# The second layer's input norm in two halves of three token tiles, with a new order of transposes and weight remainders

## The reference

```python
def rms_norm(x, g):
    xf = x.astype(jnp.float32)
    y = xf * lax.rsqrt(jnp.mean(xf * xf, axis=-1, keepdims=True) + EPS)
    return (y * g.astype(jnp.float32)).astype(x.dtype)

def pre_mod(x, g, shift, scale):
    return rms_norm(x, g) * (1 + scale) + shift

def post_add(x, y, g, gate):
    return x + gate * rms_norm(y, g)

# layer 0, last line of conv_ffn, for x and for the context xc
f = (jax.nn.gelu(a) * b) @ w_down          # 2688 -> 1024
x = post_add(x, f, ffn_post_g[0], g2)
# layer 1
h, hc = pre_mod(x, mix_pre_g[1], sh1, sc1), pre_mod(xc, mix_pre_g[1], csh1, csc1)
q, k, v = split_c(h @ w_qkv, q_g, k_g)     # 1024 -> 16 heads of q, 4 of k, 4 of v, each 64 wide
q, k = apply_rope(q, cos, sin), apply_rope(k, cos, sin)
y = global_latent_attention(q, k_all, v_all) @ w_out
```

## Time and profile before

| what | value |
|---|---|
| time, median of 3 runs | 1525.89 us (1524.79 to 1525.99) |
| the profiled execution's own time | 1522.63 us |
| its span | 1520.9 us |
| mean granted TensorE clock | 0.984 |
| busy: PE, DVE, ACT, POOL | 1439.7, 1034.6, 717.4, 568.1 us |

### The profile page before, as it was taken

The page is one execution under the profiler, slowest core; times in us unless marked ns, Lnnn a source line. Parts: engine busy times, 40 slices in busy tenths (PEclk is TensorE's granted clock), DMA queues, the critical chain, the costliest instruction groups (busy, mean ns, idle before and its releaser), DMA issues.

```text
span 1520.9 us, 21702 instructions
## 1 busy us (share of the span) xinstructions
PE 1439.7 (95%) x7514; PEld 1176.4 (77%) x7514; DVE 1034.6 (68%) x1645; ACT 717.4 (47%) x1245; POOL 568.1 (37%) x509
## 2 busy tenths in 40 slices
PE   4989899999999999999999799899999999999998
PEld 1877567778888888887787578677778888888886
DVE  2368777567688667758889778788876444445445
ACT  3333666444332333224555645688875544443222
POOL 2331545343232222321135323465543444444443
PEclk8999999999999999999999899899999999999999
DMA  8230840222465346334897222010002233333321
GB/s 353 63 98 1 294 178 29 84 98 85 133 184 153 97 138 193 110 111 127 250 249 171 80 70 70 30 41 1 1 23 76 86 107 96 97 96 112 98 96 71
DMA packets 138257, 169.16 MB, mean 111 GB/s; under 512 B 8308, under 2 KB 96632, under 8 KB 137152
## 3 DMA queue, kind: packets, MB, share of 16 engines
q1 hardware_dynamic: 132928, 159.44, 33.0%
q0 software_dynamic: 4608, 8.39, 3.3%
q10 hardware_dynamic: 640, 0.26, 0.1%
HBM read 165.94 MB, written 2.14 MB: 111 GB/s over the span
## 4 chain that ended last, share of the span: by engine, by line
PE 82%; DVE 6%; ACT 4%; DMA 4%; issue 2%; POOL 1%; SPq 0%; POOLq 0%; DVEq 0%; ACTq 0%
PE ps L560 22%; PE ps L561 22%; PE ps L562 22%; PE ps L1567 4%; PE ps L1553 4%; PE ps L1578 2%; PE ps L1580 2%; DMA start_w<-in_ada_w_dram 2%; PE ps L1461 1%; DMA fast_more<-in_ffn_w_down_dram 1%; PE ps L1053 1%; ACT prob L1609 1%; PE ps L923 1%; DMA ada_w<-in_ada_w_dram 1%; POOL prob L1740 0%
## 5 line engine op out<-in xcount | busy, mean ns | idle before, releaser
L552 POOL TENSOR_TENSOR w_lo<-raw,w_hi 128x1024 fp32r<-128x1024 f32 (+1 forms) x116 | 276.1, 2382 | 472.4 <-ACT w_hi L546 472.4
L560 PE MATMUL ps<-hT_hi,w_hi 128*128 128x512 f32 (+1 forms) x1096 | 387.4, 353 | 4.4 <-DVE hT_lo L2018 3.7
L561 PE MATMUL ps<-hT_lo,w_hi 128*128 128x512 f32 (+1 forms) x1096 | 385.0, 351 | 0.0
L562 PE MATMUL ps<-hT_hi,w_lo 128*128 128x512 f32 (+1 forms) x1096 | 382.7, 349 | 0.0
L560 PEld LDWEIGHTS ps<-hT_hi,w_hi 128*128 128x128 f32 x1096 | 207.3, 189 | 41.4 <-DVE hT_lo L2018 5.6
L562 PEld LDWEIGHTS ps<-hT_hi,w_lo 128*128 128x128 f32 x1096 | 206.5, 188 | 28.9
L561 PEld LDWEIGHTS ps<-hT_lo,w_hi 128*128 128x128 f32 x1096 | 207.1, 189 | 26.9
L546 ACT ACTIVATE w_hi<-raw 128x1024 fp32r<-128x1024 f32 (+1 forms) x137 | 142.3, 1041 | 97.4 <-PE ps L562 78.0
L1740 POOL TENSOR_SCALAR prob<-prob,small 128x768 f32<-128x768 f32 (+3 forms) x112 | 90.0, 804 | 122.1 <-DVE small L1658 122.1
L560 PE MATMUL ps<-w_hi,hT_hi 128*128 128x512 f32 (+1 forms) x288 | 110.8, 385 | 6.6 <-DVE hT_lo L895 2.9
L2321 DVE SCALAR_TENSOR_TENSOR conv_b<-ps,convw,conv_b 128x511 f32<-128x511 f32 (+1 forms) x63 | 39.7, 658 | 113.5 <-ACT conv_b L2264 113.5
(11 more groups left out here) (296 smaller groups left out, 2837.0 us busy)
## 6 DMA issues: line engine op xcount, KB each, us to landing
raw<-in_ffn_w_up_dram SPq DMA_DIRECT2D x84, 512.0 KB, 3.9
ada_w_up<-in_ada_w_dram SPq DMA_DIRECT2D x48, 512.0 KB, 4.1
ada_w<-in_ada_w_dram SPq DMA_DIRECT2D x32, 512.0 KB, 4.8
raw<-in_ffn_w_down_dram SPq DMA_DIRECT2D x56, 256.0 KB, 4.3
raw<-in_ffn_w_down_dram SPq DMA_DIRECT2D x21, 512.0 KB, 3.5
fast_more<-in_ffn_w_down_dram SPq DMA_DIRECT2D x38, 256.0 KB, 3.8
start_w<-in_ada_w_dram SPq DMA_DIRECT2D x8, 1024.0 KB, 8.4
raw<-in_ffn_w_down_dram POOLq DMA_DIRECT2D x24, 256.0 KB, 5.7
```

The source lines that it names most:

```text
L552: by.tensor_tensor(split_to(w_lo, phase, m, width), split_from(phase, m, width), split_to(w_hi, phase, m, width).bitcast(F32), ALU.subtrac ...
L560: nc.tensor.matmul(outp, s_hi, m_hi, start=first, stop=False, skip_group_check=True)
L561: nc.tensor.matmul(outp, s_hi, m_lo, start=False, stop=False, skip_group_check=True)
L562: return nc.tensor.matmul(outp, s_lo, m_hi, start=False, stop=last, skip_group_check=True)
```

## The change

- `FAST_TAIL` is 3. In ScalarE's loop `x_scaled` makes xn of tiles 0, 1 and 2 at units 69, 70 and 71. The last two units' weight blocks go to the two `fast_sub` buffers, so that SP can load weight units 0 to 2 of the projection earlier.
- The norm of layer 1 is 16 half-steps (`half_turn`, `half_scalar`, `half_vector`, `half_fill`): 8 chunks for tiles 0 to 2, then 8 for tiles 3 to 5, through two banks. ScalarE writes the high part straight from PSUM and then the scaled value in place; VectorE makes only the remainder. After each half-step PE does the matmuls of three key and value tiles. Half-steps 0 and 1 are transposed ahead of the last product's third tile.
- The first half's parts lie in `first_hi` and `first_lo` (the place of `act_g`), since `hT_hi` and `hT_lo` still hold the product's data. SP moves them into place (two moves of 1.57 MB inside SBUF) ahead of the load of unit 7; the query tiles wait for that.
- Behind the product, ScalarE, VectorE and POOL have new orders: half-steps and weight splits between the steps of the sum back into x (below). Weight remainder 0 is VectorE's, 1 to 3 stay POOL's.
- In the projection the half-steps 8 to 15 stand between the first three key tiles' work; weight remainders 4 to 7 are POOL's, each behind the power of tiles 0 to 3; 8 to 11 are VectorE's as before.
- The transposes get a table in the place of the rule, and the phase waits between norm and projection are gone.

```diff
-FAST_TAIL = 6
+FAST_TAIL = 3
+        def half_turn(pe, step):
+            half, k = divmod(step, KC)
+            if step == 0:
+                pe.wait_ge(s("norm_xn_scalar"), HALF_T)
+                pe.wait_ge(s("fast_out"), OUT_C21 + HALF_T)
+            if step == KC:
+                pe.wait_ge(s("norm_xn_scalar"), HALF_T + 1)
+                pe.wait_ge(s("norm_xn"), norm_base("mix1", "xn") + VECTOR_XN)
+            if step >= 2:
+                pe.wait_ge(s("norm_split"), norm_base("mix1", "split") + 2 * (step - 1))
+            for i in range(HALF_T):
+                mm = nc.tensor.transpose(half_bank(step)[:, i * P:(i + 1) * P],
+                                         xn[:, HALF_T * half + i, k * P:(k + 1) * P], ident[:, :])
+        def half_fill(pe, step):
+            pe.wait_ge(s("norm_split"), norm_base("mix1", "split") + 2 * (step + 1))
...
+            for i in range(HALF_T):
+                mm = mm3(acc_at(1, HALF_T * half + i, width), hi[:, tt], lo[:, tt], ...)
+        def half_scalar(act, step):
+            pieces = ((0, P, 0), (P, HTOK, 1)) if half else ((0, HTOK, 0),)
+            for dst in (half_out(step)[0], half_bank(step)):
+                for c0, c1, v in pieces:
+                    op = nc.scalar.activation(dst[:, c0:c1], half_bank(step)[:, c0:c1], ACT.Identity, ...)
+        def half_vector(dve, step):
+            nc.vector.tensor_tensor(lo, half_bank(step), hi.bitcast(F32), ALU.subtract).then_inc(s("norm_split"), 2)
 proj_sync
+                    if l and m == 7:
+                        sp.wait_ge(s("norm_split"), norm_base("mix1", "split") + 2 * KC)
+                        for whole, first in ((hT_hi, first_hi), (hT_lo, first_lo)):
+                            sp.dma_start(whole[:, :, 0:HTOK].bitcast(F32), first[:, :, :].bitcast(F32))
-        ACC_BANKS = ((0, 1), (6, 7, 4, 5, 0, 1))
-        TURN_LAG = (2, 3)
+        ACC_BANKS = ((0, 1), (6, 5, 4, 7, 0, 1))
+        TURNED_BEHIND1 = {3: (0, 1), 6: (2,), 7: (3,), 8: (4, 5), 9: (6,), 10: (7,), 11: (8, 9), 12: (10,), 13: (11,)}
 proj_tensor, layer 1
+            for step in range(HALF_STEPS if l else 0):
+                half_fill(pe, step)
+                if step + 2 < HALF_STEPS:
+                    half_turn(pe, step + 2)
+                else:
+                    turn(step + 2 - HALF_STEPS)
 proj_scalar, layer 1
+            for step in range(KC, HALF_STEPS if l else 0):
+                half_scalar(act, step)
+                if step in SUMS_AFTER:
+                    read_sums(SUMS_AFTER.index(step))
+                if step in QUERY_HI_AFTER:
+                    split_hi(act, phase, 4 + QUERY_HI_AFTER.index(step), ...)
+        SUMS_AFTER = (KC + 1, KC + 3, KC + 5)
+        QUERY_HI_AFTER = (KC + 4, KC + 6, KC + 7)
+        QUERY_LO_AFTER = {0: (4,), 1: (5,), 2: (6,), 3: (7,),}
+        QUERY_LO_VECTOR = {7: (8, 9, 10), 8: (11,)}
 proj_pool, behind the power of tile n
+                        for m in QUERY_LO_AFTER.get(n, ()):
+                            split_lo(pool, phase, m, unit_width(l, m))
 proj_vector, layer 1 (rope_first: sums, tables, halves; rope_second: factor, QUERY_LO_VECTOR, copy, remainder)
+                half_vector(dve, KC)
+                rope_gains()
+                half_vector(dve, KC + 1)
+                for n in range(HALF_T):
+                    at = rope_first(n)
+                    half_vector(dve, KC + 2 + 2 * n)
+                    if n == HALF_T - 1:
+                        half_vector(dve, KC + 3 + 2 * n)
+                    rope_second(n, at)
+                    if n < HALF_T - 1:
+                        half_vector(dve, KC + 3 + 2 * n)
 fast_tensor, behind the units before the tail
             for i in range(HALF_T):
+                if i == HALF_T - 1:
+                    half_turn(pe, 0)
+                    half_turn(pe, 1)
 fast_scalar, behind the loop
+            close(act, "act")
+            a, b, c = range(HALF_T, ALL_T)
+            whole = len(FAST) - FAST_TAIL + HALF_T
+            weights(0, 2)
+            weights(1, len(FAST) - 4)
+            half_scalar(act, 0)
+            half_scalar(act, 1)
+            second_square(a)
+            second_square(b)
+            x_square(act, "mix1", "ffnpost0", ALL_T, a)
+            second_square(c)
+            weights(2, whole)
+            half_scalar(act, 2)
+            x_square(act, "mix1", "ffnpost0", ALL_T, b)
+            x_scaled(act, "mix1", a)
+            half_scalar(act, 3)
+            x_square(act, "mix1", "ffnpost0", ALL_T, c)
+            weights(3, whole)
+            for step in range(4, KC):
+                half_scalar(act, step)
 fast_vector, behind the loop
+            split_lo(dve, "proj1", 0, unit_width(1, 0), by=nc.vector)
             for t in range(HALF_T):
                 fast_gate_early(dve, HALF_T + t)
-            x_normed(dve, "mix1", 0)
-            x_normed(dve, "mix1", 2)
+            half_vector(dve, 0)
+            half_vector(dve, 1)
             for t in range(HALF_T, ALL_T):
...
                 nc.vector.tensor_tensor(z, fast_second(t), gate[:, v, BANK:D], ALU.mult)
+                if t == ALL_T - 1:
+                    half_vector(dve, 2)
                 added(t)
...
+            half_vector(dve, 3)
+            x_normed(dve, "mix1", ALL_T - 2)
+            half_vector(dve, 4)
             x_normed(dve, "mix1", ALL_T - 1)
+            for step in range(5, KC):
+                half_vector(dve, step)
```

More of the change, by code:

```diff
@@ L434, in norm_base @@
                 return each[what] * ALL_T * len(before)
-            steps = {"mix0": KC, "ffn0": len(norm_steps(0)), "mix1": KC}
+            steps = {"mix0": KC, "ffn0": len(norm_steps(0)), "mix1": HALF_STEPS}
             each = {"turned": 1, "split": 2, "h32": 1}[what]
-            return sum(each * steps[t] * (2 if what == "h32" and t[:3] == "mix" else 1) for t in before)
-        VECTOR_XN = ALL_T - 2
+            return sum(each * steps[t] * (2 if what == "h32" and t == "mix0" else 1) for t in before)
+        VECTOR_XN = ALL_T - 4
+        HALF_STEPS = 2 * KC
         def norm_steps(l):
@@ L937, in norm_tensor, with half_bank, half_out @@
             fill(KC - 1)
+        def half_bank(step):
+            return bank(2 + step % 2, HTOK)
+        def half_out(step):
+            half, k = divmod(step, KC)
+            if half == 0:
+                return first_hi[:, k, :], first_lo[:, k, :]
+            return hT_hi[:, k, HTOK:TOK], hT_lo[:, k, HTOK:TOK]
+        def half_turn(pe, step):
+            half, k = divmod(step, KC)
+            if step == 0:
[9 more added lines that the diff above has]
+                                         xn[:, HALF_T * half + i, k * P:(k + 1) * P], ident[:, :])
+            mm.then_inc(s("norm_turned"), 1)
@@ L1084, in proj_tensor @@
                                 pe.wait_ge(s(f"qk_steps{l}"), free)
-                        for k in range(KC) if gi or batch[0] >= KV_FIRST else ():
+                        if l and gi == 1 and batch[0] == 0:
+                            pe.wait_ge(s("first_moved"), 2 * 16)
+                        for k in range(KC) if gi or l == 0 else ():
                             if batch[0] == 0 and k % 2 == 0:
@@ L2398, in fast_landed @@
                 return
-            name, before = FAST_LANDED[slot]
-            eng.wait_ge(s(name), before + 16 * (u // FAST_RAW + 1))
+            name, before = FAST_LANDED[fast_slot(u)]
+            turns = u // FAST_RAW
+            if u >= FAST_LAST:
+                turns = len(range(u - FAST_LAST, sum(FAST_SUBS), FAST_SUB))
+            eng.wait_ge(s(name), before + 16 * (turns + 1))
         def fast_source(at):
```

258 lines of the change are left out of this document (145 added, 113 removed).

## The result

| | before | after |
|---|---|---|
| time, median, four runs each | 1525.34 us (1522.86 to 1525.99) | 1536.78 us (1535.17 to 1540.09) |
| ratio, 95% interval | | 1.0081 (1.006 to 1.0101) |
| profiled execution, its span | 1522.63, 1520.9 us | 1535.17, 1533.2 us |
| mean granted TensorE clock | 0.984 | 0.983 |

The changed kernel is 11.4 us slower; 1536.5 was forecast, within 1527 to 1541. The page gives the same picture as before: 7514 matmuls, 2.7 us more busy time, 12.3 us more span.

What follows compares the result with a forecast made beforehand. TensorE, busy 95% of the span, was taken as the bound, so only its idle or half-clock stretches matter. Stage costs 2.0 - 0.2 + 8.8 = 10.6 us, added to 1525.9, gave 1536.5 us; range 1527 to 1541.

Steps and rivals of the forecast that it cites:

- The product: End of the last Strassen product: three waits, 2.1 us together against 2.9 before; TensorE through at 855.3, against 856.25.
- First half: Norm half-steps 0 to 7: TensorE idles 7.6 us before half-step 2, then loses 1.6 us at the lower clock.
- Half-step 7: Last half-step of the norm's first half: ends at 883.7, TensorE being the late engine at 2.42 us a step.
- Half-step 13: Norm's second half: tile 1's power waits behind weight remainder 4 on GpSimd; 3.5 us idle, 1.8 at lower clock.
- Up to the batch: Keys' end to the end of query tiles 7 to 9: 24.75 us, against 24.95 before.
- The order of turns: New transpose order behind the query tiles holds VectorE at tile 6; tile 13's sum of squares 8.8 us later.
- The sum: Start of tile 13's last chain: 2.0 - 0.2 + 8.8 = 10.6 us later; time 1536.5.
- Rival 1: GpSimd's remainders 3 and 5 lock out VectorE, adding 0.8 and 0.7 us on TensorE's path; 1538.0; chance 0.1.
- Rival 2: GpSimd doesn't bind half-step 13, so 3.5 and 1.8 us go; +5.3, 1531.2; chance 0.13.
- rival 4: The order of turns costs nothing, VectorE not being held at tile 6; 1528.5; chance 0.12.
- Rival 3: TensorE runs through both norm halves; keys end 13.5 us earlier, 8.6 lost in the queries; 1521.0; chance 0.06.
- What was put at nothing: Costed at nothing: two moves of first_hi and first_lo, 3.1 MB, with 28 us of cover, and removed phase waits.

Runs made afterwards that it cites:

- e2_power: Changed kernel with GpSimd's weight remainder 4 behind the power of tile 1, 5 and 6 behind that of tile 2; 1532.07 us, ratio 1.0051.
- e3_chain: Changed kernel with another order on VectorE and ScalarE behind the last product, the tile chains starting earlier; 1533.31 us, ratio 1.0055.
- e6_chain2: Changed kernel with the order of e3_chain, some half-steps moved further, and weight remainders 1 and 2 by VectorE; 1530.95 us, ratio 1.0045.
- e1_turns: Changed kernel with the old order of turns (transposes behind the query tiles); 1529.11 us, ratio 1.0033.
- e4_before_turns: Kernel before with only the new order of turns behind the query tiles; 1534.54 us, ratio 1.0067.
- v1_all: Changed kernel with e6_chain2's changes, remainders 4 to 7 by VectorE, old turns and a separate table for ScalarE's key readings; 1516.62 us, ratio 0.9951.
- e5_vec_lo: Changed kernel with weight remainders 4 to 7 by VectorE instead of GpSimd; 1532.17 us, ratio 1.0047.

## Why the prediction was right

**The product.** Through at 855.3 forecast, 855.2 measured (855.59 less its wait). The three waits are 1.79 us (0.37, 0.89, 0.53), forecast 2.1. That the instants agree so closely is in part luck: the waiting matmul that A begins with comes at 847.2 to 851.3 in the runs with this same code ahead of it. What was forecast well are the lengths between them.

**First half.** Half-step 2 forecast for 867.75, measured 867.57; chains from 855.84 (856.0), 3.77 apart (3.78). Idle 6.89 where 7.6 stood, as half-steps 0 and 1 ended 0.6 later. The clock was the lower one until 870.6, for the first 6 of the 9 matmuls where 8 were taken; in e2_power, behind the same wait, until 875.4, so this term has 1.5 us of chance in it. The reason behind it, the length of the path over VectorE, ScalarE and GpSimd, was tested by e3_chain and e6_chain2: shortened, it brings half-step 2 from 20.21 to 16.99 and 14.03 us behind the reference matmul.

**Half-step 7** ended at 883.5 (883.7). ScalarE's four activations were taken at 1.7, they take 1.60.

**Half-step 13.** Power of tile 1 done at 898.20 (898.3), matmul at 899.97 (900.1), idle 3.19 (3.5). The lower clock was put at 1.8 us; 0.71 for 3.0 us and 0.87 for 6.5 are 1.7. It fell only 1.3 us after TensorE was back at work; in e1_turns it did not fall at all behind the same wait, so that this term came true is partly luck. The queue as cause is shown by e2_power. Keys end at 908.65 (909.1), so the stage costs 1.5 us, not 2.0. The queue inversion was the right reading of an order of instructions that no row of before shows: only the durations came from rows, the order from the code.

**Up to the batch.** The wait for unit 7 is 1.14 (1.35). The batch ends at 933.97 (934.23 less 0.26), 25.3 after the keys, forecast 24.75; so this stage costs 0.4 where -0.2 stood.

**The order of turns.** Forecast +8.8 for the batch's end to tile 13's sum of squares, 36.9 us; measured 37.7, which is +9.6. Tile 10 starts about 9.1 after the batch (8.65): the mechanism is as said, with the copy of tile 6 held 7.54 us. One term was wrong in kind: the wait of 2.2 us for weight remainder 11 is 0.17. Remainder 11 was there at 948.74, within 0.3 us of the forecast (batch's end + 15.0); it was TensorE that came 1.8 us later than forecast, at 948.47, slowed by the clock. The waits of 4.66 and 1.25 brought the lower clock, 0.50 in 940 to 943 and 0.81 in 943 to 950, the last alone 0.19 x 7 = 1.3 us; with half of the 1.75 us of work in the first it is 2.2. The prediction had counted no clock loss there although it counted one behind the other two stalls. Two errors of nearly one size so cancelled. The last turns ahead of attention (976.39) took 1.97 instead of 1.09 us at the lower clock, 0.9 more that was not forecast.

**The sum.** +10.6 forecast (2.0, -0.2, 8.8); +11.45 measured at tile 13's sum of squares (1.5, 0.4, 9.6, from unrounded instants), +12.3 in span, +11.4 in the medians.

**Rival 1, VectorE locked out,** was given 0.1 and is half true. The mechanism is there. The three gate products ahead of the chains, beside remainder 1, took 4.09 us (850.90) where 1.9 would do; ScalarE had half-step 1 only at 855.19, so the chains began some 0.2 us later for it. At the rival's own places it did not lengthen the path: xn of tile 5 took 2.00 us and one operation of the halves of tile 2 took 1.15 instead of 0.29 (900.94), but TensorE was the late engine there and waited for neither. Its price shows once the larger waits are gone: 0.98 us in e2_power, 1.7 us in the first chain of e3_chain. By the Trainium skill, page "SBUF — State Buffer", section "Who interferes with whom", a VectorE instruction with two SBUF inputs and a GpSimd instruction that reads SBUF hold each other off for a whole instruction. The trace agrees, now with VectorE as the loser (0.42 to 2.37 and 2.50, 0.69 to 2.38), where the earlier trace rows had only GpSimd.

**Rival 2** (GpSimd doesn't bind half-step 13) and **rival 4** (the turns cost nothing) are excluded by e2_power and by e1_turns and e4_before_turns. **Rival 3** (TensorE runs through both halves) was given 1521.0, with the turns' loss in it. In the changed kernel the two stalls exclude it. v1_all, with the turns mended, goes a good half of its way: from the product's end to the end of the keys the rival counted 38.3 us, v1_all takes 43.6, before took 50.9. It needed, as the rival said, other chains than the earlier trace rows, not a faster engine. What was put at nothing (the moves of `first_hi` and `first_lo`, the removed phase waits) is named by no wait in the trace; no run took it out by itself.

## What to carry to other kernels

Before work is moved to an engine with time to spare, read what stands behind it in that engine's queue and who waits for that; here a remainder of 2.4 us ahead of a power of 1.2 us cost 4.9 us with the clock in the profiled execution, and 4.6 in the medians with the four remainders given back (e5_vec_lo). A change of order that frees nothing by itself (the turns, 10.4 us on the old kernel) should be run alone before it goes into a larger change. And when a stall is costed, count the lower clock behind each one, not only behind the longest, as a range: behind one and the same wait of 3.2 us it cost 1.7 us or nothing.

## What the runs showed of the hardware

- A VectorE operation on SBUF that meets GpSimd's remainder of 128x1024 ends 0.2 to 0.6 us after the remainder does, however short it is alone: 0.42 to 2.37 and 2.50, 0.69 to 2.38 us. It is not only operations on two tensors: the CAST of a key tile at 906.84 took 2.23 instead of 0.29, and xn by VectorE 1.52 and 2.00 in the changed kernel and 1.40 for tile 5 in v1_all, each beside a remainder, against 0.74 for tile 4 in v1_all, which met none.
- VectorE does the same remainder in 1.2 us (2.35 for two), and GpSimd's 2.4 us can cost VectorE up to 2.1 us (0.42 to 2.50). With GpSimd's share given back, v1_all has VectorE busy for 1029.0 us, the changed kernel for 1031.2.
- The granted clock fell from 2.4 to 1.2 GHz only 1.3 us after TensorE was back from the wait of 3.19 us, and in e1_turns about 1.0 us after a wait of only 1.80 us. Behind the same wait (3.2 us before half-step 13) it fell 0.1 us after work began in e3_chain, 1.2 us in e6_chain2, and not at all in e1_turns. In v1_all, with waits up to 1.39, it did not fall between 856 and 956.
- Behind the wait of 6.9 us before half-step 2, TensorE worked at the lower clock for 3.0 us in the changed kernel and for up to 5.9 us in the others (e2_power): the same wait costs 1.5 or 3.0 us of lower clock.
- ScalarE's split of weight unit 11 in the changed kernel waited 2.27 us for its load, which SyncE could issue only when VectorE had freed the slot; it cost nothing, since VectorE came later still.
